# The first modulation blocks of a two-layer encoder: weights prefetched, one half summed by TensorE, one pair of bias products

## What is computed

```python
c_act = jax.nn.silu(c)
for l in range(DEPTH):
    mod = (c_act @ w_ada[l] + b_ada[l])[:, None, :]          # (1, 6 * 1024)
    sh_a, sc_a, g_a, sh_m, sc_m, g_m = jnp.split(mod, 6, axis=-1)
    h = x * (1.0 + sc_a) + sh_a
    proj = h @ w_in[l]
    ...
bias = jnp.moveaxis(rel_bias[t5_bucket(off * dilation)], -1, 0)   # 4 heads, shared by the layers
```

## Time and profile before

| | us |
|---|---|
| median of three runs | 1500.44 |
| the profiled execution | 1502.46 |
| its span, first to last instruction | 1500.7 |
| TensorE busy | 1348.9 |
| VectorE busy | 1054.1 |
| ScalarE busy | 599.4 |
| GpSimd busy | 294.4 |
| first transpose of X | 43.81 |
| first product of the first chunk | 49.13 |

### The profile page before, as it was taken

How to read it: one execution, slowest core, us unless ns; L and a number is a source line. 1 busy time by engine, 2 the same in 40 slices (tenths; PEclk the granted TensorE clock), 3 DMA queues, 4 the chain that set the end, 5 groups by cost and what they waited for, 6 DMA issues and landing times.

```text
span 1500.7 us, 23220 instructions
## 1 busy us (share of the span) xinstructions
PE 1348.9 (90%) x6728; PEld 1126.7 (75%) x6728; DVE 1054.1 (70%) x1830; ACT 599.4 (40%) x1216; POOL 294.4 (20%) x312
## 2 busy tenths in 40 slices
PE   5998987799899999999959898869989999999992
PEld 2897866687688887878759877758778878788772
DVE  6667699877688465565765878979675865565578
ACT  0356387661532122222144647868153222222121
POOL 0031075220125000000410404723010700000024
PEclk9999999899999999999979998989989999999996
DMA  8854700004233333334236462010423333233421
GB/s 298 291 180 159 223 8 14 26 15 151 82 126 125 120 119 119 95 118 151 71 131 202 154 205 69 1 38 1 141 81 123 127 119 119 91 126 121 146 98 56
DMA packets 92131, 174.14 MB, mean 116 GB/s; under 512 B 8124, under 2 KB 18748, under 8 KB 92024
## 3 DMA queue, kind: packets, MB, share of 16 engines
q1 hardware_dynamic: 91496, 170.79, 34.8%
q10 hardware_dynamic: 528, 2.10, 0.4%
HBM read 168.66 MB, written 4.19 MB: 115 GB/s over the span
## 4 chain that ended last, share of the span: by engine, by line
PE 58%; DVE 15%; DMA 10%; issue 9%; ACT 5%; POOL 2%; SPq 1%; DVEq 0%; ACTq 0%; POOLq 0%
PE bank L1303 18%; PE bank L1305 18%; PE bank L1304 18%; DMA slab_raw<-in_w_in 5%; DVE ada_sum L820 2%; DMA ada_w<-in_w_ada 2%; DMA slab_raw<-in_w 1%; PE bank L1332 1%; DVE pt_lo L1060 1%; DVE smax L1047 1%; PE bank L1470 1%; DVE X L1088 1%; DVE tmp L1085 1%; DVE k_lo L1018 1%; DMA band<-bias_rows 1%
## 5 line engine op out<-in xcount | busy, mean ns | idle before, releaser
L1303 PE MATMUL bank<-hT_hi,slab_hi 128*128 128x512 f32 x576 | 224.5, 390 | 2.8 <-ACT kB L640 2.8
L1305 PE MATMUL bank<-hT_hi,slab_lo 128*128 128x512 f32 x576 | 224.2, 389 | 0.0
L1304 PE MATMUL bank<-hT_lo,slab_hi 128*128 128x512 f32 x576 | 224.1, 389 | 0.0
L1303 PE MATMUL bank<-slab_hi,h_hi 128*128 128x512 f32 x512 | 203.8, 398 | 5.6 <-ACT mod_a L791 5.6
L1304 PE MATMUL bank<-slab_lo,h_hi 128*128 128x512 f32 x512 | 202.3, 395 | 0.0
L1305 PE MATMUL bank<-slab_hi,h_lo 128*128 128x512 f32 x512 | 202.1, 395 | 0.0
L1140 DVE TENSOR_TENSOR slab_lo<-slab_raw,slab_hi 128x512 fp32r<-128x512 f32 x240 | 178.3, 798 | 22.5 <-ACT slab_hi L774 15.6
L820 DVE SCALAR_TENSOR_TENSOR ada_sum<-ada_w,c_col,ada_sum 128x512 f32<-128x512 f32 x196 | 153.3, 782 | 24.3 <-DMA ada_w<-in_w_ada 20.2
L1303 PE MATMUL bank<-slab_hi,hT_hi 128*128 128x384 f32 (+3 forms) x448 | 152.8, 341 | 14.1 <-ACT tmp L535 5.4
L1305 PE MATMUL bank<-slab_hi,hT_lo 128*128 128x384 f32 (+3 forms) x448 | 151.5, 338 | 0.0
L1304 PE MATMUL bank<-slab_lo,hT_hi 128*128 128x384 f32 (+3 forms) x448 | 151.4, 338 | 0.0
(11 more groups left out here) (197 smaller groups left out, 2605.5 us busy)
## 6 DMA issues: line engine op xcount, KB each, us to landing
slab_raw<-in_w SPq DMA_DIRECT2D x256, 256.0 KB, 2.7
ada_w<-in_w_ada SPq DMA_DIRECT2D x56, 1024.0 KB, 5.9
slab_raw<-in_w_in SPq DMA_DIRECT2D x48, 192.0 KB, 4.8
slab_raw<-in_w_o SPq DMA_DIRECT2D x32, 256.0 KB, 2.7
slab_raw<-in_w_in SPq DMA_DIRECT2D x16, 256.0 KB, 3.4
band<-bias_rows SPq DMA_DIRECT2D x8, 448.0 KB, 3.2
slab_raw<-in_w_in SPq DMA_DIRECT2D x16, 144.0 KB, 4.4
X<-in_x SPq DMA_DIRECT2D x1, 2048.0 KB, 10.3
```

Of the source, the lines that this page charges most:

```text
L1303: pe.matmul(dst, a_hi, w_hi, start=first, stop=False)
L1304: pe.matmul(dst, a_hi, w_lo, start=False, stop=False)
L1305: return pe.matmul(dst, a_lo, w_hi, start=False, stop=last)
```

## The change

Only the head of the program is rewritten, with what it feeds:

- A tile `ada0` holds all eight halves of the first four blocks. SP issues their loads without a wait, in the order 0, 1, 7, 2, 3, 4, 5, 6, behind onehot and lncnt (which goes to 4 partitions instead of 128), and X right after them. The biases of the four blocks come as 16 columns (`bcol`).
- VectorE sums seven halves (`first_sum`), the first piece of each block a plain product. TensorE forms the eighth, half 7, itself: 16 products with c as the moving column into bank 7.
- The bias rows are one pair of products with rel itself as weights: `frow` is 4 partitions (a head each) by 1024. The store to the scratch names each row 128 times. It is issued as soon as VectorE has added lncnt to the two halves, behind the first block.
- VectorE writes `aff` from PSUM with the bias columns; ScalarE's four copies go. TensorE waits for `aff_ready` between ln0 and ln1.
- ropeT and ropeK are loaded behind the wait for `aff_ready`, ahead of growrow, and again in each layer.

```diff
-        relb = over("relb", [32, 4, P], 0)
-        lncnt = over("lncnt", [P, 1024], 8192)
-        frow = over("frow", [P, 4, 1024], 12288)
+        lncnt = over("lncnt", [4, 1024], 8192)
+        frow = over("frow", [4, 1024], 12288)
+        ada0 = over("ada0", [P, 2 * AHEAD, KT // 2, 512], 28672)
...
+            sp.dma_start(onehot[:, :], t_in["onehot"]).then_inc(table_in, 16)
+            sp.dma_start(lncnt[:, :], t_in["lncnt"].broadcast_to([4, 1024])).then_inc(table_in, 16)
...
+            for m in (0, 1, 7, 2, 3, 4, 5, 6):
+                b, half = divmod(m, 2)
+                src = t_in["w_ada"][0, 512 * half:512 * half + 512, 512 * b:512 * b + 512]
+                sp.dma_start(ada0[:, m, :, :], src.rearrange("(k p) n -> p k n", p=P)).then_inc(ada0_in[m], 16)
+                if m == 7:
+                    sp.dma_start(bcol[:, :], t_in["b_ada_col"]).then_inc(bcol_in, 16)
+            sp.dma_start(X[:, :, :], t_in["x"].rearrange("(t p) d -> p t d", p=P)).then_inc(x_in, 16)
             sp.wait_ge(setup_pool, 1)
-            for n in range(2 * AHEAD):
-                if n >= 2:
-                    sp.wait_ge(ada_half, n - 1)
-                ada_load(0, slice(512 * (n // 2), 512 * (n // 2) + 512), n % 2)
...
                         sp.dma_start(colpack[:, :], t_in["colpack"][l]).then_inc(small_in, 16)
+                        sp.dma_start(ropeT[:, :, :], t_in["ropeT"]).then_inc(const_in, 16)
+                        sp.dma_start(ropeK[:, :, :, :], t_in["ropeK"]).then_inc(const_in, 16)
...
-            for b in range(AHEAD):
-                act.wait_ge(mod_ready, b + 1)
-                act.activation(mod_a[:, 4 * b:4 * b + 4], bank[b][:, 0:4], ACT.Copy,
-                               bias=float(b >= 2)).then_inc(setup_act, 1)
-
-            act.wait_ge(setup_dve, 2 + 4)
-            act.dma_start(scratch.rearrange("h p n -> p h n"), frow[:, :, :]).then_inc(band_out, 16)
+            act.wait_ge(rows_done, 2)
+            act.dma_start(scratch, frow[:, :].unsqueeze(1).broadcast_to([4, P, 1024])).then_inc(band_out, 16)
...
+            def first_sum(b):
+
+                dst = ada_sum[:, b, :]
+                last = KT // 2 if b == AHEAD - 1 else KT
+                for k in range(last):
+                    if k % 4 == 0:
+                        dve.wait_ge(ada0_in[2 * b + k // 4], 16)
+                    w, c = ada0[:, 2 * b + k // 4, k % 4, :], c_col[:, 1, k:k + 1]
+                    if k == 0:
+                        ins = dve.tensor_scalar(dst, w, c, None, ALU.mult)
                     else:
-                        dve.wait_ge(dve_step, 2 + 6 * blk + k - k // 4)
-                    ada_piece(k, blk).then_inc(ada_half if k % 4 == 3 else dve_step, 1)
...
+            first_sum(0)
+            dve.wait_ge(table_in, 32)
+            for j in range(2):
+                at = slice(512 * j, 512 * j + 512)
+                dve.wait_ge(setup_pe, j + 1)
+                dve.tensor_tensor(frow[:, at], bank[4 + j][0:4, :], lncnt[:, at], ALU.add).then_inc(rows_done, 1)
+            first_sum(1)
+            first_sum(2)
+            dve.wait_ge(bcol_in, 16)
+            dve.wait_ge(ada0_cols, 1)
+            dve.scalar_tensor_tensor(out=mod_a[:, 12:16], in0=bank[7][:, 4:8], scalar=1.0, in1=bcol[:, 12:16],
+                                     op0=ALU.add, op1=ALU.add).then_inc(mod_part, 1)
+            first_sum(3)
...
+            dve.wait_ge(mod_ready, 4)
+            dve.tensor_tensor(aff[:, 0, 0, 4:8], bank[7][:, 0:4], mod_a[:, 12:16], ALU.add).then_inc(aff_ready, 1)
...
+            for j in range(2):
+                pe.matmul(bank[4 + j][0:4, :], rel[:, :], onehot[:, 512 * j:512 * j + 512], start=True, stop=True
+                          ).then_inc(setup_pe, 1)
+            pe.wait_ge(setup_dve, 1)
+            pe.wait_ge(ada0_in[2 * AHEAD - 1], 16)
+            for c in range(4):
+                for k in range(4):
+                    ins = pe.matmul(bank[7][:, 4 + c:5 + c], ada0[:, 2 * AHEAD - 1, k, P * c:P * c + P],
+                                    c_col[:, 1, 4 + k:5 + k], start=k == 0, stop=k == 3)
+            ins.then_inc(ada0_cols, 1)
+            pe.wait_ge(rows_done, 2)
             for b in range(AHEAD):
-                pe.wait_ge(setup_dve, 2 + b)
-                pe.matmul(bank[6][:, :], relb[:, b, :], onehot[:, 0:512], start=True, stop=True)
-                pe.matmul(bank[7][:, :], relb[:, b, :], onehot[:, 512:1024], start=True, stop=True
-                          ).then_inc(setup_pe, 1)
-                pe.wait_ge(ada_half, 2 * b + 2)
-                mod_cols(bank[b], ada_sum[:, b, :])
+                pe.wait_ge(ada0_sum, b + 1)
+                if b == AHEAD - 1:
+                    pe.wait_ge(mod_part, 1)
+                mod_cols(bank[4 + b], ada_sum[:, b, :])
...
                 transpose_x("ln0", 0)
+                pe.wait_ge(aff_ready, l * 2 + 1)
                 transpose_x("ln1", 0)
```

More of the change, by code:

```diff
@@ L145, in trunk @@
         tmp = keep("tmp", [P, 2, S])
+        bcol = keep("bcol", [P, 16])
         u0 = cursor[0]
@@ L222, in trunk @@
         ada_in = [sem(f"ada_in{i}") for i in range(2)]
+        ada0_in = [sem(f"ada0_in{i}") for i in range(2 * AHEAD)]
+        bcol_in, rows_done, ada0_sum, ada0_cols, mod_part = map(
+            sem, ("bcol_in", "rows_done", "ada0_sum", "ada0_cols", "mod_part"))
         band_in, band_out, stored = sem("band_in"), sem("band_out"), sem("stored")
@@ L822, in ada_piece @@
                     in1=ada_b[:, :] if k == 0 else dst, op0=ALU.mult, op1=ALU.add)
-            dve.wait_ge(rel_in, 16)
-            dve.tensor_copy(relb[:, :, :], rel[:, :].unsqueeze(2).broadcast_to([32, 4, P])).then_inc(setup_dve, 1)
-            for blk in range(AHEAD):
-                for k in range(KT):
+            def first_sum(b):
[5 more added lines that the diff above has]
+                    w, c = ada0[:, 2 * b + k // 4, k % 4, :], c_col[:, 1, k:k + 1]
@@ L839, in _ @@
-                dve.tensor_tensor(frow[:, blk, 0:512], bank[6][:, :], lncnt[:, 0:512], ALU.add)
-                dve.tensor_tensor(frow[:, blk, 512:1024], bank[7][:, :], lncnt[:, 512:1024], ALU.add
-                                  ).then_inc(setup_dve, 1)
-            dve.wait_ge(setup_act, 1 + AHEAD)
-            dve.tensor_copy(aff[:, 0, 0, :], mod_a[:, 8:16])
-            dve.tensor_copy(aff[:, 0, 1, :], mod_a[:, 0:8]).then_inc(aff_ready, 1)
+                        ins = dve.tensor_scalar(dst, w, c, None, ALU.mult)
+                    else:
+                        dve.wait_ge(dve_step, 2 + (KT - 1) * b + k)
+                        ins = dve.scalar_tensor_tensor(out=dst, in0=w, scalar=c, in1=dst, op0=ALU.mult, op1=ALU.add)
@@ new lines, in first_sum @@
+                    ins.then_inc(dve_step if k < last - 1 else ada0_sum, 1)
+            first_sum(0)
[8 more added lines that the diff above has]
+            dve.wait_ge(ada0_cols, 1)
@@ new lines, in _ @@
+            dve.scalar_tensor_tensor(out=mod_a[:, 12:16], in0=bank[7][:, 4:8], scalar=1.0, in1=bcol[:, 12:16],
+                                     op0=ALU.add, op1=ALU.add).then_inc(mod_part, 1)
+            first_sum(3)
+            for b in range(2):
+                dve.wait_ge(mod_ready, b + 1)
+                dve.tensor_tensor(aff[:, 0, 1, 4 * b:4 * b + 4], bank[4 + b][:, 0:4], bcol[:, 4 * b:4 * b + 4], ALU.add)
+            dve.wait_ge(mod_ready, 3)
+            dve.scalar_tensor_tensor(out=aff[:, 0, 0, 0:4], in0=bank[6][:, 0:4], scalar=1.0, in1=bcol[:, 8:12],
+                                     op0=ALU.add, op1=ALU.add)
@@ L882, in ada @@
                     if k % 4 == 0:
-                        dve.wait_ge(ada_in[k // 4], (l * NBLK + AHEAD + n + 1) * (32 if k == 0 else 16))
+                        dve.wait_ge(ada_in[k // 4], (l * NBLK + n + 1) * (32 if k == 0 else 16))
                         dve.wait_ge(ada_half, l * 2 * NBLK + 2 * (AHEAD + n) + k // 4)
@@ L1178, in ada_next @@
                         dve.wait_ge(mod_ready, l * NBLK + b + NBLK)
-                    dve.wait_ge(ada_in[u], (l * NBLK + b + (NBLK + 1)) * (16 if u else 32))
+                    dve.wait_ge(ada_in[u], (l * NBLK + b + (NBLK - AHEAD + 1)) * (16 if u else 32))
                     dve.wait_ge(ada_half, l * 2 * NBLK + b * 2 + (2 * NBLK + u))
```

24 lines of the change are left out of this document (6 added, 18 removed).

## The result

| | us | ratio to before, 95% interval |
|---|---|---|
| before, median of 4 | 1500.54 | |
| after, median of 4 (1550.01 to 1552.87) | 1551.09 | 1.0349 [1.0328, 1.0371] |

A forecast was written before the change was run, and what follows sets the result against it. TensorE was taken as full (90% of span), so only the head before the first product could move. A slow store blocking slab 8 onward summed +61.8, +2.8, less 5 to +59.6: 1562 us from 1502.5, range 1496 to 1574.

The forecast's parts named there:

- -11.3: Head of the program: loads ahead and shorter sums start the transposes of X at 32.5 instead of 43.81 us.
- 84.2 us: Bias rows' store: duration taken, 512 x 0.1645 us, if four neighbouring partitions deliver only 25 GB/s; other end 21.1 us.
- Transfers are served in order of issue across the two queues: DMA queues: a crawling store, placed behind slab 7 (35.7 to 119.9 us), stops all behind it; slab 8's product +61.8 us.
- the variant at 1567 with +65: Store gets in between the weight halves, so all that follows waits: −11.3 + 84.2 − 8 = +65, 1567 us.
- +59.6: Sum for the slow, blocking store: slab 8's product +61.8, slabs 9 and 10 +2.8, less 5; 1562 us, chance 0.52.
- the forecast's hole: TensorE idle between the first and second chunk (about 70 us), waiting for slab 8 behind the slow store.
- Nothing later moves: Behind the head: products follow without a hole and nothing later hangs on absolute time, so no gain there.
- an earlier slab gains nothing: Slab loads of the first chunks: DMA only 0.40 busy from 66 to 82 us, so earlier slabs bring nothing.
- price of up to +2: ropeT and ropeK loaded again in layer 1, where VectorE's first cast waits: 0 taken, bounds 0 and +2 us.
- Full rate on four engines: Rival: the store runs on four engines at full rate, costing 21.1 us of everybody's time; 1507 us, chance 0.19.
- an even spread: Rival: the store is spread over 16 engines or its engines don't matter, 5.3 us; 1493 us, chance 0.19.
- Slow but holding up nobody: Rival: store lands at 99.4 us, delaying only ScalarE's bank clearing and the third chunk, +19; 1521 us, chance 0.10.

The follow-up runs named there:

- late: The changed kernel with its bias rows' store issued only once aff is ready, behind the wait for X; 1552.72 us.
- late_dve8: s128_late with VectorE summing all eight halves, loaded in order 0 to 7, without TensorE's 16 column products; 1498.39 us, 0.9975 of before.
- b_s4: The kernel before, its store reading only partitions 0 to 3, each row 128 times (bias rows of heads 1 to 3 left out); 1571.77 us.
- s128: The changed kernel with bias rows made on 128 partitions (32 per head) and stored from all, each four times, by 16 engines; 1486.76 us, 0.9915 of before.
- b_quarter: The kernel before, storing only head 0's bias rows (0.5 MB instead of 2.1), which all heads read; 1496.85 us, 0.9982 of before.
- b_pad8: The kernel before with eight tiny copies that do no needed work at the start of VectorE; 1494.47 us, 0.9956 of before.
- s4spread: The changed kernel with bias rows on 16 partitions, only partitions 0, 4, 8 and 12 stored, each row 128 times, by four engines; 1499.63 us.
- late_rope: s128_late with ropeT and ropeK loaded once, ahead of the first slabs, as in before; 1485.54 us, 0.9911 of before.
- s128_late: s128 with its store issued only once aff is ready, behind the wait for X; 1487.25 us, 0.9934 of before.

## Why the prediction was right, and where it was not

**The head.** `late` runs it without a store beside it and shows each step: first piece 7.89 (predicted 7.8), sum 0 to 13.9 (13.8), bias rows to 15.1 (15.1), sum 1 to 22.0 (21.6), sum 2 to 28.0 (27.5), sum 3 to 30.8 (30.5), aff at 32.9 (32.7), transposes at 32.67 (32.5). The 16 column products took 6.95 us (7.5) and were covered. The k = 0 pieces took 0.49 us, between the bounds of 0.415 and 0.752. So the -11.3 were right, and VectorE is the bound of that head (late_dve8: four pieces more, 3.1 us).

**The store.** The number of engines (516 packets, four) and the slow source were right. 84.2 us was taken, 87.9 measured from issue to the last packet (87.6 in `late`, 86.9 in b_s4). In part that is luck: a row took 0.558 us, not the 0.658 behind the 84.2, which makes 71.4 us for the 128 rows of an engine; the rest is the start (the first packet is seen at 19.5) and the loads' turns on the same engines. The 76 us, an estimate by the 27.6 GB/s of the Trainium skill (SBUF — State Buffer, section "Door 1: The DMA port swizzle"), lies between the two.

**What it holds up: the step that failed.** "Transfers are served in order of issue across the two queues", so the store would stand behind slab 7 and leave the halves alone. It did neither. SP's timeline in after:

```profile
4.96 10.09 SPq L312 DMA_DIRECT2D ada<-in_w_ada  x5
15.09 7.00 SPq L315 DMA_DIRECT2D X<-in_x  x1
22.55 62.87 SPq L320 DMA_DIRECT2D slab_raw<-in_w_in  x8
```

All eight halves were issued by 15.05, before the store, and still sum 2's second half came 19.13 us late: the store's packets began at 19.5, and loads issued ahead of it were still landing at 45.7, 67.8 and 90.4. Nor had SP by 15.2 issued "everything up to the slabs": X's issue ran to 22.09, and the eight slabs' to 85.42 (18.34 to 28.11 in `late`, with no store beside them). There was no hole between the first and second chunk. I had named this as the variant at 1567 with +65. With 87.9 us for the store instead of 84.2 it would be +68.6 (-11.3 + 87.9 less 8 of overlap), but the first product moved by +57.7: X and two slabs came through while the store still ran, so the overlap was 18.9 us and not 8. A place that was wrong, an overlap of twice the size and a gain behind the first product (below) happened to leave the time, +48.5, within the range around +59.6. The row that misled me was that of three microseconds with packets of q10 alone; why nothing else moved there is open. The Trainium skill had the rule that I should have weighed, in DMA: Bandwidth & Descriptors, section "Queues, rings and completion order": each DMA engine takes turns between the queues that have work for it. After's trace (151 packets of q1 beside 60 of q10 from 30 to 40 us) and s128's landing (12.2 us instead of the 8.6 of before) agree; the three microseconds don't. The place of the forecast's hole is seen after all in `late`, where the store is issued behind the slabs and TensorE stands idle between the first and second chunk; its order isn't, since slab 8 came at 93.24 and the store ended at 120.7.

**"Nothing later moves".** The sum gave the rest of the kernel no gain; it was 9.2 us shorter. By the timelines 3.3 us are gained before the mixer's end in layer 0 (330.2 us after the first product in before, 326.9 in after). Without the old store at 44 us, slabs 12 to 15 are no longer late, which is worth 3.1 us in b_quarter; in after 2.5 us of that went at once, as its first 96 products ran in part at the low clock (19.3 us instead of 16.7), so that it is only 0.8 us ahead behind the four chunks (65.2 against 66.0). Another 2.5 us come in the 9 us after that, where TensorE waits for VectorE's cst (once, 3.26 us, instead of 1.33 and 3.26); why is not traced, and that 3.3 is so near to 3.1 is in part chance. 3.9 us are gained at the start of layer 1 (10.65 against 6.79), by the place of VectorE's code (b_pad8: 3.9). Some 2 us lie in small pieces of layer 1 and are not traced. For the slabs, "an earlier slab gains nothing" was read from a window (66 to 82 us) that ended just ahead of the hole. For layer 1 I did name the wait and a code fetch, with a price of up to +2; the sign was open and I took one side.

**The rivals.** Full rate on four engines (1507) and an even spread (1493) needed a source that isn't slow: s4spread (1499.6) and s128 (1486.8) are their kernels, 7 and 6 us below what the rivals' sums gave, which left out the gain behind the first product. Slow but holding up nobody (1521) fell with after itself, where the halves came late, and with the slabs of `late`.

The profiled run adds up: 1502.5 + 57.7 - 9.2 = 1551.0.

## What to carry to other kernels

A broadcast from a few neighbouring partitions saves an engine's work and pays in DMA time: let the source of a large store stand on many partitions (here one tiny copy, two products of full width and 1.7 us for a wider table), and judge a transfer by what the busiest engine spends on it, which is about what the loads beside it were late here. When a change moves the number of instructions ahead of a loop, measure it again with a few idle ones added: 4 us of a difference may be the place of the code. s128 is the version to keep (0.9915; late_rope's 0.9911 can't be told from it), and what bounds it next, by s128_late, are the transfers of the first 60 us.

## What the runs showed of the hardware

- A group of four neighbouring partitions gave 29 to 32 GB/s to stores, by 4 or by 16 engines (table above); partitions 0, 4, 8 and 12 fed one engine each at its full 26.
- Beside one slow store on four engines, the loads of all 128 partitions on another queue first went on (358 GB/s from 16 to 30 us, both together, the store's packets from 19.5) and then fell to 66 GB/s for 60 us (46 to 78), while the store took 89% of the time of four engines (30 to 40 us). That the loads wait for their packets on these four engines was only argued, since the trace does not tell engines apart.
- The granted clock of TensorE was 0.53 (1.2 GHz for most of it) from 98 to 112 us in after, behind 60 us with 3.7 us of work at 1.00 and 5.5 us of transposes, also at 1.00, and with 5.1 us of work in these 14 us; a product of 384 columns then took 0.52 us, and 0.33 once it was back at 1.00.
- Eight instructions of VectorE at the program's head moved a wait of 3 to 4 us at the loop's second turn, in either direction; that it waits for code is argued from its place alone.
